# Low pass before high pass in a streamed two-pass product kernel on Trainium2

## What is computed

```python
def squared_relu_mlp(h, w_up, w_down):
    return jnp.square(jax.nn.relu(h @ w_up)) @ w_down
...
    for layer in range(DEPTH):
        hn = rmsnorm(h, norm_mix_pre[layer])
        ...
        h = h + rmsnorm(mix, norm_mix_post[layer])
        f = squared_relu_mlp(rmsnorm(h, norm_mlp_pre[layer]), w_up[layer], w_down[layer])
        h = h + rmsnorm(f, norm_mlp_post[layer])
```

## Time and profile before

| what | value |
|---|---|
| median of 3 runs | 3093.16 us (3093.05 to 3094.21) |
| the profiled execution | 3091.55 us, span 3089.8 us, mean granted clock 0.993 |
| PE busy, matmuls | 3022.1 us, 98% of the span, 17715 matmuls |
| DVE busy | 2189.8 us, 71% |
| ACT busy | 1458.1 us, 47% |
| POOL busy | 283.8 us, 9% |
| transfers | 548.28 MB, mean 177 GB/s; 49.0% of 16 engines' span |

### The profile page before, as it was taken

The page is one execution under the profiler, slowest core; times in us unless marked ns, Lnnn a source line. Parts: engine busy times, 40 slices in busy tenths (PEclk is TensorE's granted clock), DMA queues, the critical chain, the costliest instruction groups (busy, mean ns, idle before and its releaser), DMA issues. The chain is left out here.

```text
span 3089.8 us, 48135 instructions
## 1 busy us (share of the span) xinstructions
PE 3022.1 (98%) x17715; PEld 2658.4 (86%) x17715; DVE 2189.8 (71%) x2926; ACT 1458.1 (47%) x1842; POOL 283.8 (9%) x191
## 2 busy tenths in 40 slices
PE   8999999999999999999999999999899999899997
PEld 7888888888888888888888888888788888788887
DVE  6776775767666687765856666676879865879764
ACT  5334544434334555545533333344656545656453
POOL 0002300000001400004100000002300004100003
PEclk9999999999999999999999999999999999999999
DMA  6555455555555444445455554555444435344444
GB/s 238 182 185 191 164 191 187 186 187 189 189 190 190 150 177 171 170 162 192 164 190 190 190 190 176 199 186 188 155 160 173 155 134 204 137 177 152 162 151 176
DMA packets 76554, 548.28 MB, mean 177 GB/s; under 512 B 8480, under 2 KB 8992, under 8 KB 10656
## 3 DMA queue, kind: packets, MB, share of 16 engines
q1 hardware_dynamic: 76448, 546.81, 49.0%
HBM read 544.68 MB, written 2.10 MB: 177 GB/s over the span
## 5 line engine op out<-in xcount | busy, mean ns | idle before, releaser
L773 ACT ACTIVATE w_high<-raw 128x2048 fp32r<-128x2048 f32 x506 | 965.5, 1908 | 1102.3 <-DMA raw<-stream 1101.5
L287 PE MATMUL acc<-xs,w_high 128*128 128x512 f32 x4947 | 1243.8, 397 | 14.6 <-ACT w_high L924 9.0
L1192 DVE TENSOR_TENSOR w_low<-raw,w_high 128x2048 fp32r<-128x2048 f32 x506 | 1155.8, 2284 | 95.1 <-ACT w_high L773 92.7
L287 PEld LDWEIGHTS acc<-xs,w_high 128*128 128x128 f32 x4947 | 910.9, 189 | 202.1 <-ACT w_high L924 9.0
L287 PE MATMUL acc<-inner,w_high 128*128 128x512 f32 x2976 | 715.2, 391 | 0.0
L294 PE MATMUL acc<-xs,w_low 128*128 128x256 f32 x4962 | 686.0, 284 | 0.0
L294 PEld LDWEIGHTS acc<-xs,w_low 128*128 128x128 f32 x4962 | 657.9, 193 | 23.2
L287 PEld LDWEIGHTS acc<-inner,w_high 128*128 128x128 f32 x2976 | 546.1, 188 | 105.1 <-issue 0.7
L1211 DVE TENSOR_REDUCE y<-acc 128x256 f32<-128x512 f32 x406 | 279.7, 689 | 485.4 <-PE acc L294 484.4
L294 PEld LDWEIGHTS acc<-inner,w_low 128*128 128x128 f32 x2976 | 383.0, 191 | 15.4
L294 PE MATMUL acc<-inner,w_low 128*128 128x256 f32 x2976 | 387.8, 283 | 0.0
(11 more groups left out here) (163 smaller groups left out, 1365.9 us busy)
## 6 DMA issues: line engine op xcount, KB each, us to landing
raw<-stream SPq DMA_DIRECT2D x514, 1024.0 KB, 4.8
h<-x_t SPq DMA_DIRECT2D x4, 512.0 KB, 7.8
out<-h SPq DMA_DIRECT2D x4, 512.0 KB, 2.6
raw<-stream SPq DMA_DIRECT2D x2, 512.0 KB, 7.0
consts<-tables SPq DMA_DIRECT2D x1, 960.0 KB, 16.5
branch<-w_spatial SPq DMA_DIRECT2D x1, 512.0 KB, 17.2
branch<-b_spatial SPq DMA_DIRECT2D x1, 512.0 KB, 18.1
prob_t<-lambdas SPq DMA_DIRECT2D x1, 256.0 KB, 18.2
```

What stands on the lines that cost most here:

```text
L287: nc.tensor.matmul(acc[s][:, :], w_high[:, s, kt * P:(kt + 1) * P], x[:, kt, :, :], start=(kt == first_of[0]), stop=False, skip_group_chec ...
L773: nc.scalar.activation(w_high[:, s, 0:units * P], raw[:, s, 0:units * P], ACT.Copy)\
L1192: V.tensor_tensor(w_low[:, s, 0:units * P], raw[:, s, 0:units * P], w_high[:, s, 0:units * P], ALU.subtract).then_inc(low_ready, 1)
```

## The change

1. `product` waits for `low_ready` at its start, runs the 16 low matmuls first (the first of them clears the bank) and the 16 high ones after them; the wait for `high_ready` is gone, since `low` has waited for it. The last low matmul raises a new semaphore `low_passed`. Hooks are renumbered by `in_order` (0 to 8 become 0 to 16, 9 to 15 become 17 to 23 of 32). `product_first`, `product_early`, `product_last` and the latent products keep their order.
2. SyncE's loop is written out: `load(c)` waits for `low_passed` of chunk c - 4 where that chunk is an ordinary product, and for `product_done` where it is in the set `LOW_LAST`.
3. `high` waits for `product_done` of chunk c - 4 as well, since the transfer no longer implies it.
4. The two halves of the third chunk become one piece each: `ahead` on ScalarE ahead of the last square, and on VectorE ahead of the last product's result.
5. In `norm_input` `high(c + 3, 3)` moves from behind the ninth block to the end.

```diff
+SECTIONS = (C_MLP0, C_QKV, C_MLP1, C_LAYER2, C_LAYER2 + N_LAYER2)
+LOW_LAST = ({0} | {c + s for c in SECTIONS + tuple(OUT_CHUNKS + DOWN_CHUNKS) for s in range(3)} | set(LATENT_CHUNKS)
+            | {c - 1 for c in SECTIONS} | {CHUNKS - 1})
...
-            with sp.Fori(1, LOADED // 4) as i:
-                for s in range(4):
-                    sp.wait_ge(product_done, 4 * i + (s - 3))
-                    load(4 * i + s, s)
-            for c in range(LOADED - LOADED % 4, LOADED):
-                sp.wait_ge(product_done, c - 3)
+            passed = 0
+            for c in range(4, LOADED):
+                if c - 4 in LOW_LAST:
+                    sp.wait_ge(product_done, c - 3)
+                else:
+                    passed += 1
+                    sp.wait_ge(sem("low_passed"), passed)
                 load(c, c % 4)
...
-                pe.wait_ge(high_ready, c + 1)
+                hooks = {in_order(kt): hook for kt, hook in (hooks or {}).items()}
+                pe.wait_ge(low_ready, c + 1)
                 pe.wait_ge(summed, at(c - 3))
-                first_of[0] = 0
-                for kt in range(units):
-                    if hooks and kt in hooks:
-                        hooks[kt]()
-                    if ready:
-                        ready(kt)
-                    high_unit(s, kt, x)
-                pe.wait_ge(low_ready, c + 1)
-                for kt in range(units):
-                    mm = low_unit(s, kt, x, kt == units - 1)
+                for i in range(2 * units):
+                    if i in hooks:
+                        hooks[i]()
+                    kt = i % units
+                    if i < units:
+                        mm = low_unit(s, kt, x, False, start=(kt == 0))
+                        if kt == units - 1:
+                            mm.then_inc(sem("low_passed"), 1)
+                    else:
+                        mm = nc.tensor.matmul(acc[s][:, :], w_high[:, s, kt * P:(kt + 1) * P], x[:, kt, :, :],
+                                              start=False, stop=(kt == units - 1), skip_group_check=True)
                 mm.then_inc(product_done, 1)
+
+            def in_order(kt):
+
+                return 2 * kt if kt <= KB // 2 else KB // 2 + kt
...
                 act.wait_ge(landed[s], (c - s) * 4 + 16)
+                if not isinstance(c, int) or c > 3:
+                    act.wait_ge(product_done, c - 3)
...
-                    if b == KB // 2:
-                        high(c + 3, 3)
+                high(c + 3, 3)
...
                     if more:
-                        high_half(c0 + b + AHEAD, 0)
+                        ahead(c0 + b, s)
                     square(acc[s][:, 0:TOKENS], squares_post(m) + b, s,
                            lambda: act.wait_ge(product_done, c0 + b + 1))
-                    if more:
-                        high_half(c0 + b + AHEAD, 1)
...
+                            if isinstance(b, int) and b == KB - 2:
+                                ahead(c + 1, s + 1)
                             gain(m, b)
...
-                if c is not None:
-                    low_half(c + 2, m, 0)
                 mean(r, D, NORM_EPS, "square_added", squares_post(m) + KB)
-                if c is not None:
-                    low_half(c + 2, m, 1)
...
+                if more:
+                    ahead(c0 + KB - 1, 3)
...
+                        ahead(c, 3)
                         dve.wait_ge(product_done, c + 1)
```

More of the change, by code:

```diff
@@ L777, in ahead @@
                 high(c + AHEAD, (s + AHEAD) % 4, units)
-            def high_half(c, part):
-                act.wait_ge(landed[2], (c - 2) * 4 + 16)
-                a, b = part * UNITS * P // 2, (part + 1) * UNITS * P // 2
-                nc.scalar.activation(w_high[:, 2, a:b], raw[:, 2, a:b], ACT.Copy)\
-                    .then_inc(high_ready if part else sem("high_begun"), 1)
             def square(src, k, s, ready):
@@ L1196, in ahead @@
                 low(c + AHEAD, (s + AHEAD) % 4, units)
-            def low_half(c, m, part):
-                if part:
-                    dve.wait_ge(high_ready, c + 1)
-                else:
-                    dve.wait_ge(sem("high_begun"), m + 1)
-                a, b = part * UNITS * P // 2, (part + 1) * UNITS * P // 2
-                op = V.tensor_tensor(w_low[:, 2, a:b], raw[:, 2, a:b], w_high[:, 2, a:b], ALU.subtract)
-                if part:
-                    op.then_inc(low_ready, 1)
             def sum_halves(c, s, to=None):
```

13 lines of the change are left out of this document (7 added, 6 removed).

## The result

The changed kernel takes **3105.35 us** (median of 6 runs, 3104.84 to 3109.9) against 3093.36 us (6 runs, 3091.61 to 3094.6) for the kernel before on the same chip: 12.0 us more, a ratio of 1.0043 (95% interval 1.0033 to 1.0053). The forecast was 3102.9 (3096 to 3108). The profiled execution took 3105.62 us, span 3103.9, mean granted clock 0.991; TensorE's matmuls are busy 3026.8 us of it. The spans of the two profiled executions differ by 14.1 us: the kernel before was profiled in an execution of 3091.55 us, 1.8 us under its median.

The account below looks back on a forecast made before the run. TensorE's matmuls fill 98% of the span, so only its own list counts. Terms 5.6 + 1.6 + 2.4 - 3.9 + 1.3 + 2.7 make +9.7 us, from 3093.16 to 3102.9 us, range 3096 to 3108.

Parts of the forecast that it names:

- Steady products: Products in a steady stretch: transfer and need of the low part both move 3.65 us earlier, so 0 change.
- c+3: Fourth chunk of five sections: its high part moves last on ScalarE, its low part delays the statistic, +0.55 us each.
- c+4 of the MLP sections: Fifth chunk of both MLP sections: TensorE waits for VectorE's low part, +2.8 us each, 5.6 in all.
- c+4 of the attention section: Fifth chunk of the dilated attention: starts 2.8 us late, scores 1.6 late; +1.6 us, plus 0.9 for a slow low pass.
- c+4 of the two layers: Fifth chunk of the two last layers: late start partly covered by VectorE's list, +1.2 us each, plus 0.9 each for the clock.
- the first bank some 0.5 later: Two last layers: first score bank ready at 2665.8, 0.5 us after scores start, so only 1.1 to 1.2 passes on.
- The clock in the MLP sections: Fifth-chunk waits of 2.5 us in the MLP sections: too short for a clock fall, 0, at most 0.9 us.
- Third chunk in one piece: Ends of three out sections: early transfer finishes the split before the last product ends, -1.3 us each, -3.9 in all.
- The 0.2 and 0.2 ahead of the mean: Out section ends: mean no longer behind a half low part, last square behind a half high part, 0.2 us each.
- End of the MLP sections: Ends of two MLP sections: GpSimd's add slips between two low parts, last result late, +0.65 us each, 1.3 in all.
- Start of the kernel: Second product waits 2.3 us for its low part, but the statistic's 3.64 us wait covers it: 0.
- Late transfers: Rival: written-out loads still issue late, a late third chunk blocks the last square at five seams; 3111 us, chance 0.03.

Follow-up runs that it names:

- five_low: Against the changed kernel, low pass first and early transfer kept only in the product before the last of each section before a norm; 3089.94 us.
- late: Changed kernel with every transfer behind the whole product again, low-first order and one-piece split kept; 3123.38 us.
- c34_high: Changed kernel with the fourth and fifth chunk of each section back to high pass first, their successors' transfers behind the whole product; 3088.1 us.
- middle: Changed kernel with ScalarE's high part of the section's fourth chunk back in the middle of the norm's inputs; 3108.96 us.
- filled: Changed kernel with 11 extra thrown-away high matmuls ahead of the low-part wait at each section's fifth chunk; 3098.87 us.
- halves: Changed kernel with the third chunk at each section end split in halves again, its transfer still early; 3104.27 us.
- seam_filled: The kernel of c34_high plus ten thrown-away matmuls in TensorE's idle time at each of the five section ends before a norm; 3087.44 us.

## Why the prediction was right, step by step

- **Steady products, 0: right in the MLP sections, not quite in the layers.** Their rest is 1.29 and 0.59 us faster in the changed kernel, and about as much in every version but five_low (-0.39 and -0.10) and the rest of layer 1 in late, whose 0.84 holds the mean that comes 2.07 us later. It was in no term.
- **c+3, +0.55 each: the mechanism right, the size 0.4.** The statistic waits for the low part of c+3 (in three of five starts by the changed kernel's list); c34_high takes that away and gains 0.3 to 1.0 us at each seam. The later high part on ScalarE gives 0.4 to 0.6 of it back (middle). Net, the seams behind the MLP sections are 0.40 and 0.38 us longer, and those behind the out sections 0.38 to 0.47 once the power's 0.93 is added to -0.55, -0.53 and -0.46. (In the forecast 361.05 + 2.28 is 363.33, not 363.35, which changes nothing.)
- **c+4 of the MLP sections, +2.8 each, 0.55 of it from c+3: right.** The waits are 2.74 us. Past the seam the stretches grow by 2.31 to 2.75 us where no fall comes in (late apart), some 0.3 of it at their ends, against 2.25.
- **c+4 of the attention section, 1.6 and 0.9 for the clock: right.** Past the seam 1.88 us, where 2.5 - 0.55 - 0.4 (the mean of the out section) = 1.55 was forecast. Without the fall it is 0.57 (filled) against 0.65, so the clock's part is 1.3, not 0.9.
- **c+4 of the two layers, 1.2 and 0.9 for the clock: too small, the largest miss.** Past the seam 2.75 and 2.85 us, where 2.1 - 0.55 = 1.55 was forecast. The clock alone is 1.0 and 1.3 (filled), near the 0.9; at full clock 1.73 and 1.56 are left, where 0.65 was forecast. The step that failed is "the first bank some 0.5 later". The last layer, in the kernel before, the changed one and filled:

```profile
2663.70 1.00 PE L416 MATMUL score<-k_t,q_t 64*128 64x128 f32 x8 [1.01 <-DVE k_t L1353]
...
2677.26 1.57 PE L430 MATMUL score<-k_t,q_t 64*128 64x128 f32 x8
...
2678.86 0.56 DVE L1353 SCALAR_TENSOR_TENSOR prob<-score,consts 128x384 f32<-128x384 f32 x1 [2.72 <-PE score L430]
...
2671.06 0.93 PE L437 MATMUL score<-k_t,q_t 64*128 64x128 f32 x8
...
2672.02 0.56 DVE L1363 SCALAR_TENSOR_TENSOR prob<-score,consts 128x384 f32<-128x384 f32 x1 [1.43 <-PE score L437]
```

VectorE takes up the first bank 0.96 us behind the start of the scores at full clock (filled) and 1.6 at half clock (changed kernel). It took it up 0.99 behind in the kernel before too (2663.70, and 2664.69 in the earlier trace rows), so VectorE's own list, on which I had counted for cover, held nothing back there: with 0.99 in place of 0.5 all of the scores' 1.6 us pass on, not 1.1 to 1.2. VectorE now stands still for 2.72 us at that place. Then c+5 waits 0.76 us for its low part, which was in no term.

- **The clock in the MLP sections, 0: wrong in part.** "Shorter than anything after which the rows show a fall" was a rule from one row, and the trace of the kernel before speaks against it: its clock falls at about 341.8 us, 0.6 us behind the wait of 2.16 us of the earlier trace rows. A wait of 2.74 us is followed by a fall in 3 of the 10 cases (two MLP sections in the five profiles with this order and no filling) and costs 1.4 us then; with a wait of 3.8 or 3.9 us there is a fall in all 15, in 8 of them before the wait has ended.
- **Third chunk in one piece, -1.3 each: the gain of the power as I said (1.63 to 0.70), its cause half right.** The -0.55 of a seam holds the power's -0.93 and c+3's +0.4 together. The 0.2 and 0.2 ahead of the mean did not come in the first out section (-0.06 in all). And halves shows that the early transfer, which the forecast names too, does it, and the one piece adds nothing there. So each of the three gave 0.9, not 1.3.
- **End of the MLP sections, +0.65 each: too large.** The result is 0.28 us later (the forecast's own 1061.3 was 0.7 behind 1060.60). By the row of 5.03 us GpSimd did slip in between the two low parts; the other case, 0.1 with the two back to back, did not come. The rule of the Trainium skill, page "SBUF — State Buffer", section "Who interferes with whom", that whoever is first has the port pair for its whole instruction, agrees with the earlier trace rows and halves: begun 0.16 us behind VectorE's half the power takes 1.63 us (1.06 to the half's end and 0.57), begun 0.04 us ahead of it 0.70.
- **Start of the kernel, 0: the step "3.64 us cover it" is half right.** The new wait is covered (2.35 us in the second product, and the statistic's falls from 3.64 to 1.41). But the slow stretch that a wait used to cover can now land behind it, and is then worth 1 to 2 us; the profiles show both.
- **Late transfers, 3111 as a rival: too mild**, 3123.

Added up in the profiled executions: the layers' starts +2.5 against the forecast, the start of the program +2.0, the two MLP sections +1.0 (a fall +1.4, their ends less), the end +0.5, the attention +0.3 and the first stage +0.3; on the other side the rest of the layers -1.5, the out sections' seams -0.4 and the MLP sections' -0.3. That is +4.4, the 14.1 of the spans against 9.7. By the medians it is 12.0; 1.8 of the 2.1 us between the two is that the kernel before was profiled in an execution that much under its median, so some of the +4.4, at the start perhaps, is that execution's luck. The sign, the places and the range held. The sum is 2.3 us short, and it came that near with errors on both sides: the layers' 2.5 too little against the rest of the layers, which was in no term.

## What to carry to other kernels

Turning two passes round moved little time in the steady stream (-1.3 and -0.6 us in the rest of the two layers), but it puts the part that is made last at the front: look for the few products that follow a burst, where the helper engine is behind, and keep the old order there. A wait on TensorE costs its length and, here for 3.8 us each time and for 2.7 us in 3 of 10, another 1.0 to 1.4 us at half clock, unless another wait behind covers that. Early transfers showed a gain at the three seams behind the out sections (0.9 us each, the power), and 705.7 us less of idle time on ScalarE were worth nothing by themselves.

## What the runs showed of the hardware

- In 8 of the 15 waits of 3.8 or 3.9 us the clock fell while TensorE still stood idle, in the other 7 up to 1.0 us after; with 11 matmuls in the wait it did not fall (filled).
- Work whose result is thrown away kept TensorE's clock at 2.4 GHz: 55 matmuls made the kernel 6.5 us faster (filled). Where the time is set by another engine, holding the clock was worth under 1 us by the medians (seam_filled).
- The same instructions at the start of the program differ by about 2 us between executions (0.13 in filled, 1.96 in the changed kernel, 2.25 in middle), with the stretch at 1.2 GHz beginning at 32 us in the first and at 37 or 38 in the others.
- A start 0.20 us earlier or later against a VectorE subtraction decides between 0.70 and 1.63 us for GpSimd's power. Why GpSimd got in between two VectorE instructions that stand one behind the other in the list, no run here tells.
